# A two-lane recurrence in a transformer kernel: both lanes' levels in one go on TensorE, and a head's sum of squares beside the next head's output

## What is computed

```python
q = silu(q); f = lb + (1 - lb) * sigmoid(f_raw); k = 1 - f; v = i_in   # 8 heads of 128
S_t = diag(f_t) S_{t-1} + k_t v_t^T;   o_t = S_t^T q_t                 # all 272 tokens
o = o * rsqrt(mean(o * o) + 1e-6) * w_norm                             # per head
y_a = o * silu(g_out);  y_b = b_gate * dwconv(c_gate * x_conv)
h = h + (sigmoid(gate_a) * y_a + sigmoid(gate_b) * y_b) @ w_out
```

## Time and profile before

| | |
|---|---|
| median of 3 runs | 1136.73 us (1136.13 to 1136.94) |
| the profiled execution | 1137.76 us, its span 1136.5 us |
| TensorE | busy 1120.5 us (99%), 10518 matmuls |
| VectorE | busy 836.0 us (74%) |
| ScalarE | busy 633.2 us (56%) |
| granted TensorE clock | full in every slice after the first |
| stretch 743 to 760 us | TensorE busy 14.77 of 17, VectorE 12.95 |
| stretch 760 to 790 us | TensorE 30.00 of 30, VectorE 25.01, ScalarE 14.57 |
| stretch 790 to 812 us | TensorE 22.00 of 22, VectorE 16.54, ScalarE 13.23 |

### The profile page before, as it was taken

One profiled execution on the slowest core, in us unless ns is written; L12 is line 12 of the kernel. 1 busy time (PEld: TensorE's weight loads), 2 busy tenths in 40 slices (PEclk: granted clock), 3 DMA queues, 4 the chain that ended last, 5 costly groups with the idle time before them and its releaser, 6 DMA issues.

```text
span 1136.5 us, 24962 instructions
## 1 busy us (share of the span) xinstructions
PE 1120.5 (99%) x10518; PEld 1074.4 (95%) x10518; DVE 836.0 (74%) x1431; ACT 633.2 (56%) x1085; POOL 71.4 (6%) x96
## 2 busy tenths in 40 slices
PE   8999999999999999999999999999999999999998
PEld 5998899999998999999999999989999999999987
DVE  5688689988886888898575589577565777666643
ACT  3587556544444777666445456735645566555532
POOL 0200013000012000111000104100000000000000
PEclk9999999999999999999999999999999999999999
DMA  9977845899997634368755634733345463664540
GB/s 340 360 238 261 297 149 186 296 319 320 313 310 259 224 116 131 120 193 261 257 178 175 205 112 149 258 115 113 112 149 186 149 223 119 197 214 161 200 167 37
DMA packets 194671, 232.09 MB, mean 204 GB/s; under 512 B 4099, under 2 KB 169571, under 8 KB 194560
## 3 DMA queue, kind: packets, MB, share of 16 engines
q1 hardware_dynamic: 193712, 230.19, 60.9%
q0 software_dynamic: 576, 0.18, 0.1%
q10 hardware_dynamic: 272, 0.14, 0.0%
HBM read 229.43 MB, written 1.05 MB: 203 GB/s over the span
## 4 chain that ended last, share of the span: by engine, by line
PE 96%; DVE 3%; issue 1%; DMA 0%; ACT 0%; DVEq 0%; POOLq 0%
PE ps L154 94%; PE ps L157 2%; DVE hL L196 1%; DMA PI<-in_positions_dram 0%; DVE LT L187 0%; DVE T L196 0%; DVE wlo L187 0%; DVE T L187 0%; DVE ANG L196 0%; ACT hH L166 0%; DVE LT L193 0%; ACT LT L166 0%; DVE LT L196 0%; DVE hL L187 0%; DVE XA L192 0%
## 5 line engine op out<-in xcount | busy, mean ns | idle before, releaser
L187 DVE TENSOR_TENSOR wlo<-raw,whi 128x1024 fp32r<-128x1024 f32 (+1 forms) x346 | 408.6, 1204 | 154.0 <-ACT whi L166 152.7
L154 PE MATMUL ps<-hH,whi 128*128 128x256 f32 (+3 forms) x1792 | 516.2, 288 | 3.8 <-DVE hL L196 1.9
L154 PE MATMUL ps<-hL,whi 128*128 128x256 f32 (+3 forms) x1792 | 504.0, 281 | 0.0
L154 PE MATMUL ps<-hH,wlo 128*128 128x256 f32 (+3 forms) x1792 | 503.6, 281 | 0.4 <-DVE wlo L187 0.3
L166 ACT ACTIVATE whi<-raw 128x1024 fp32r<-128x1024 f32 (+1 forms) x346 | 348.8, 1033 | 185.8 <-PE ps L154 134.5
L154 PEld LDWEIGHTS ps<-hH,whi 128*128 128x128 f32 x1792 | 336.9, 188 | 10.8 <-issue 5.3
L154 PEld LDWEIGHTS ps<-hH,wlo 128*128 128x128 f32 x1792 | 337.1, 188 | 0.8 <-DVE wlo L187 0.8
L154 PEld LDWEIGHTS ps<-hL,whi 128*128 128x128 f32 x1792 | 337.4, 188 | 0.4
L154 PE MATMUL ps<-uL,whi 128*128 128x256 f32 x352 | 99.2, 282 | 0.0
L154 PE MATMUL ps<-uH,whi 128*128 128x256 f32 x352 | 99.0, 281 | 0.0
L154 PE MATMUL ps<-uH,wlo 128*128 128x256 f32 x352 | 98.4, 279 | 0.0
(11 more groups left out here) (321 smaller groups left out, 1600.3 us busy)
## 6 DMA issues: line engine op xcount, KB each, us to landing
MW<-in_w_mod_dram SPq DMA_DIRECT2D x47, 1024.0 KB, 6.6
raw<-in_w_up_dram SPq DMA_DIRECT2D x44, 1024.0 KB, 5.5
raw<-in_w_in_dram SPq DMA_DIRECT2D x36, 1024.0 KB, 5.0
raw<-in_w_down_dram SPq DMA_DIRECT2D x27, 1024.0 KB, 5.4
raw<-in_w_gate_dram SPq DMA_DIRECT2D x22, 1024.0 KB, 7.6
raw<-in_w_in_odd_dram SPq DMA_DIRECT2D x12, 1024.0 KB, 6.3
raw<-in_w_in_even_dram SPq DMA_DIRECT2D x8, 1024.0 KB, 6.2
raw<-in_w_down_dram SPq DMA_DIRECT2D x8, 768.0 KB, 6.8
```

Of the source, the lines that this page charges most:

```text
L154: return self.queued(self.e.matmul(out, lhsT, rhs, start=start, stop=stop, skip_group_check=True, **kw), length if pos is None else max(le ...
L187: return self.queued(self.e.tensor_tensor(out, a, b, op), 0.07 + cols(out) / self.RATE)
```

## The change

Level `lv` of lane 0 is queued only when lane 1 has also reached level `lv`, and lane 1's block follows it with no wide matmul between. `k.level` and its distance of 2.4 are gone. In the heads, `attended(h + 1)`, the output of the next head, is queued directly behind the sum of squares of head `h`; all four values `k.v` of the lane are awaited ahead of the first.

```diff
--- before.py
+++ after.py
@@ -2037,7 +2037,7 @@
         project(P.value[s], 0, value, s, s == 0)
     for s in range(4):
         project(P.query[s], 14, query, s)
-    k.level = 0.0
+    k.grown, k.begun_level = {}, set()
     lanes = [start(k, recur(k, i, VC)) for i in range(2)]
 
 
@@ -2182,9 +2182,16 @@
         wide = L2 if lv < 4 else 256
         b = banks[1 - lv % 2]
         ps = m.ps[b]
-        yield max(due(grown), read_out(k, b), k.level)
-        while pe.clock < k.level:
-            yield k.level
+        k.grown[lane, lv] = max(due(grown), read_out(k, b))
+        if lane == 0:
+            while (1, lv) not in k.grown:
+                yield None
+            yield max(k.grown[0, lv], k.grown[1, lv])
+        else:
+            while lv not in k.begun_level:
+                yield None
+            yield k.grown[1, lv]
+        k.begun_level.add(lv)
         fill(k, b)
         pe.wait_ge(*grown)
 
@@ -2204,7 +2211,6 @@
             for h in range(4):
                 pe.mm(ps[0:M0, 128 + h * 8:128 + h * 8 + 8], K[:, h, 256:272], later(Q[:, h, 256:272]), False, True)
         weights = pe.inc()
-        k.level = pe.clock + 2.4
         yield due(weights)
         yield from spare(k)
 
@@ -2269,18 +2275,23 @@
     weights = act.inc(k.bank[b1])
     yield due(weights)
     pe.wait_ge(*weights)
-    for h in range(4):
+    o = p0[:, 0:258]
+
+    def attended(h):
         j = 4 * lane + h
         V = m.VAB[:, :, j * 128:j * 128 + 128]
-        while k.v[j] is None:
-            yield None
-        o = p0[:, 0:258]
-        yield read_out(k, b0)
         fill(k, b0)
         pe.wait_ge(*k.v[j])
         pe.mm(o, V[:, 0, :], W[:, h, 14:272], True, False)
         pe.mm(o[:, 114:258], V[:, 1, :], W[:, h, 272:416], False, False)
-        out = pe.mm(o[:, 242:258], VC[:, j * 128:j * 128 + 128], CC[:, h, :], False, True).inc()
+        return pe.mm(o[:, 242:258], VC[:, j * 128:j * 128 + 128], CC[:, h, :], False, True).inc()
+
+    while None in k.v[hs]:
+        yield None
+    yield max(read_out(k, b0), due(*k.v[hs]))
+    out = attended(0)
+    for h in range(4):
+        j = 4 * lane + h
         yield due(out)
         OT, sq = m.T[:, j, 14:], SQ[h % 2]
         act.wait_ge(*out)
@@ -2288,9 +2299,11 @@
             act.wait_ge(*k.o[j - 2])
         square = act.act(sq, o, ACT.Square).inc()
         copied = act.act(OT, o, ACT.Copy).inc(k.bank[b0])
-        yield max(due(square), read_out(k, b1))
+        yield max(due(square, copied), read_out(k, b1))
         fill(k, b1)
         mean = pe.wait_ge(*square).mm(p1[:, 0:258], m.ones[:, 2, :], sq, True, True).inc()
+        if h < 3:
+            out = attended(h + 1)
         yield due(mean)
         act.wait_ge(*mean).act(sq, p1[:, 0:258], ACT.Ln, bias=m.eps[:, 1:2]).inc(k.bank[b1])
         rstd = act.settle().act(sq, sq, ACT.Exp, scale=-0.5).inc()
```

## The result

| | before | after |
|---|---|---|
| median, us | 1136.43 (4 runs, 1136.02 to 1136.94) | 1145.53 (4 runs, 1145.17 to 1148.93) |
| ratio, 95% interval | | 1.0079 (1.0066 to 1.0092) |
| profiled execution, us | 1137.76 (span 1136.5) | 1148.93 (span 1147.7) |
| mean granted clock of TensorE, share of full | 1.000 | 0.990 |

The change makes the kernel slower by 9.1 us in the medians and by 11.2 in the two spans. The forecast was 1137.4 us, with a range up to 1140.9. So the result lies outside, on the slower side.

What follows compares the result with a forecast made beforehand. TensorE, busy 1120.5 of 1136.5 us, was taken to bound the kernel. The terms 0 - 1.2 + 2.1 + 0.5 - 0.7 = +0.7 us, added to the median 1136.73, gave 1137.4 us, range 1133.6 to 1140.9.

Steps and rivals of the forecast that it cites:

- What bounds the kernel now: Whole kernel: TensorE bounds it, 96% of the chain; its two recurrence holes, 2.2 us, are it running out of instructions.
- The first instruction hole: Start of the recurrence: hole one and the first merge are gained, then given back waiting until 754.29; taken as 0.
- Merges: Level pairs: each saves a 0.20 us change into small fp32 matmuls and back; seven 1.4 us, the remaining six -1.2.
- VectorE: Level pairs: TensorE waits for both lanes' totals, 0.24, 0.96 and 0.94 us ahead of pairs 3, 4 and 5; +2.1 together.
- The walk: Pair-by-pair reckoning, from the profile's rows, of when VectorE's totals and TensorE reach each pair; it gave +2.1 us.
- the signs named: If right: one hole of 2 to 3 us, waits near 1 us at levels 4 and 5, VectorE's waits at 1-4 gone.
- Later holes: Recurrence past 754 us: a late fetch makes a hole near pair 3 or 4, mostly under VectorE's waits; +0.5, between 0 and 3.
- instruction starvation: Rival, chance 0.20: pairs outrun instruction fetch; two holes beyond the counted waits give +4 to +5, 1141 us.
- Heads: Heads: six sums of squares with an fp32 output behind them save 0.12 us each; -0.7, ends 0 and -1.2.
- Sum: All terms together: 0 - 1.2 + 2.1 + 0.5 - 0.7 = +0.7 us, added to the median, 1137.4 us.

Runs made afterwards that it cites:

- Spaced_only: The kernel before with the levels' distance of 2.4 modelled us also around each lane's own block, heads as before: 1135.18 us, 0.9985.
- heads_only: The kernel before with only the heads' change, a sum of squares together with the next head's output, levels as before: 1137.03 us, 1.0002.
- hole_wide: The kernel before with TensorE waiting once for nine GpSimd memsets amid wide matmuls near 850 us: 1140.5 us, 1.003.
- levels_only: The kernel before with only the change's level pairs, the heads as before: 1143.84 us, 1.0057.
- Load_late: The changed kernel with the weight load of 748 to 752 us held back until the pair of level 0 is done: 1140.56 us, 1.0036.
- pairs_kind: The changed kernel, pairs adjacent, with the weight load held back and 12 wide matmuls ahead of ab, ac and every head's step: 1139.25 us, 1.0022.
- spread: The changed kernel with 12 wide matmuls between lane 0's and lane 1's level blocks: 1142.76 us, 1.0044.
- tail_apart: As spread, with 12 wide matmuls also ahead of ab, ac and each head's output and sum: 1138.36 us, 1.0011.
- hole_small: The kernel before with TensorE waiting once for nine GpSimd memsets directly behind lane 0's block of level 3, near 766 us: 1139.75 us, 1.0029.
- hole_short: The kernel before with TensorE waiting once for four GpSimd memsets amid wide matmuls: 1138.02 us, 1.0009.

## Why the prediction was wrong, by its own steps

**What bounds the kernel now**: right as far as it went. TensorE's row sets the time, and the holes are missing instructions. Spaced_only shows the latter by what it does: with more wide matmuls between the small ones both holes go. The view I never put to use is the clock's. The table ahead has it at full, and I treated it as a constant of the kernel, though it depends on the order of the work, which was exactly what the change touched. Neither the sum nor any rival has a term for it. **This is the step that failed**: I took the wide matmuls to start 0.12 us apart throughout, and for 19.3 us they started 0.217 apart. That is 8.7 of 10.4 us in the profile, and by estimate 6 of 9.1 in the median.

**The first instruction hole** (taken as 0): right in time and length, in the profile. I had TensorE stop at 751.5 and resume at 754.29 after 2.8 us. It stopped at 752.28 and resumed at 754.88, 2.60 us, and these are 751.5 and 754.1 without the 0.76 that after starts late. The DMA queues show the weight load in front (packets, MB, share of 16 engines; window 750 to 751, then 752 to 752.6):

```profile
q1 hardware_dynamic: 372, 0.38, 108.0%
...
q1 hardware_dynamic: 161, 0.15, 77.6%
q8 instruction: 1, 0.02, 11.4%
```
The weights' queue holds over 100% of the engines' time from 750 on. The instructions' piece moves as its last packets do, and TensorE goes on some 2.3 us later, as in the earlier trace rows. But a hole of 2.6 us isn't worth the same as two holes of 1.28 and 0.95. The half clock begins inside it at 753.8 and lasts until 760.6. Behind the hole 5.7 us of it are left, and 5.7 x 0.45 = 2.6 us follow that before's two holes did not bring. The 0 was also reckoned against the holes of before's profile and then added to a median. Against an execution of before with one hole of 0.7 us, as in heads_only and hole_wide, the same step would cost some 1.5.

**Merges** (-1.4 for seven): right in size, rather low. A pair of 144 small matmuls takes 751.30 - 749.77 = 1.53 us from start to next start, where two blocks took 0.81 each and a change of 0.20 between. That saves 0.29 instead of 0.20. If every pair did so, the seven would be -2.0 and the clock's part of the 10.4 us would be 9.3.

**VectorE** (+2.1): the mechanism right, the size off, 0.8 measured. The walk made TensorE wait ahead of a *pair* for both lanes' totals. In fact lane 0's block starts with its own, and only lane 1's waits. In level 3 lane 0's block starts at 768.92 without waiting, and lane 1's at 770.20 after 0.41. The block in front takes 0.8 us of every wait I had walked. By that alone level 3's 0.24 would be nothing and level 4's 0.96 would be 0.2 or so. They are 0.41 and 0.37, because VectorE was also slower than in the walk. Its rows in after, its start on pair 2 (TensorE started that at 764.65) and lane 1's totals:

```profile
766.52 0.73 DVE L187 TENSOR_TENSOR Qg<-Qg,Fg 128x544 f32<-128x544 f32 x1
...
769.76 0.29 DVE L187 TENSOR_TENSOR LB<-Fg 128x136 f32<-128x136 f32 x1
```
It began 1.87 us behind the pair's start where I had 1.22, and the totals came after 5.40 where I had 4.58. Level 5's wait of 0.94 is absent, and TensorE had spent a hole of 1.22 us and 3.4 us at half clock on the way there. In levels_only, at full clock there, it is 0.39. Of the signs named, the waits stood at levels 3 and 4 with 0.4 us each, not at 4 and 5 with 1. VectorE's own waits vanished ahead of levels 2 to 4 but not ahead of level 1, where it stood 4.80 us, the first hole and the half clock behind it on the way.

**Later holes** (+0.5): mis-sized, 0.70 + 1.22 us measured. I had laid them under VectorE's waits, and they lie beside them. The rival of *instruction starvation*, with two holes beyond the counted waits, had the places right but priced a hole at its own length, 1141 us in all. Load_late shows what that rival is worth at the full clock: 4.6 us of holes, a span of 1137.4.

The Trainium skill (Runtime: NRT & Kernel Launch, Instruction fetch mechanics) calls crossing into the next block of instructions mostly hidden. By that rule all three holes of after, and both of before, would be nought. The runs show 2.2 us in before, 4.5 in after and none in spaced_only, so for blocks of small matmuls this close it doesn't hold.

**Heads** (-0.7): mis-sized, hardly anything measured (1.0002 with an interval of 0.001 either way; 1135.04 against 1135.18 us; 0.15 us between the heads of heads_only and before, matmul against matmul). And a cost that no step named: outputs and sums in one piece make the tail denser. Levels_only's profile has the full clock there, after's doesn't.

**Sum.** Of its terms 0 - 1.2 + 2.1 + 0.5 - 0.7 = +0.7, the profiles give about 0 - 1.2 + 0.8 + 1.9 - 0.2 = +1.3, and pairs_kind's recurrence +0.9. VectorE's term was 1.3 too high and that of the later holes 1.4 too low, and it is luck that they nearly cancel. Against the medians the sum was low even without the clock: pairs_kind is +1.9 at equal clock. So of the miss of 8.1 us (1145.5 against 1137.4) the missing term, the clock, is some 6. Another 1.2 is what pairs_kind shows beyond my sum. The last 1 us or so is open, and after's longest hole and its waits, of which pairs_kind has less, may be in it.

## What to carry to other kernels

Where TensorE sets the time and is near full use, an edit that moves small matmuls together is to be priced twice: by the holes it makes, and by the granted clock behind them, which is read from the clock column in windows and from the distance of two equal matmuls. The mean clock of each execution (here one thousandth was 1 us) tells it without a trace, and executions of two kernels are best compared at equal clock. One profile shows one execution: the holes of the same order were 2.2 us in one and 0.7 in another. In these runs small matmuls did best dealt out between wide ones; if a stretch must be dense, try it with 12 wide ones between steps before giving it up.

## What the runs showed of the hardware

- The granted clock falls to half without any idle time of TensorE: 10.2 us at 0.50 in spread, behind 44.4 us of unbroken work, where small fp32 steps stand three wide matmuls apart. With 12 ahead of each step (tail_apart's profile) it stays at 1.00. Three of spread's twelve executions kept 1.000 with the same tail. The Trainium skill (TensorE: Matmul & The Clock Gate, Why this matters for your kernels) warns of idle gaps between bursts of matmuls. By that alone this stretch would have kept its clock; here the measurement decides.
- Holes of 2.60 us (after), 2.40 (spread), 2.35 (levels_only) and 2.18 (hole_wide) had a stretch at half clock in or behind them, of 3.4 to 6.8 us. Holes of 2.18 (hole_small) and 2.02 (tail_apart) had none. One of 1.88 us in the same work had it in one of thirteen profiles. In before, hole_short and load_late, holes of up to 1.3 us had the full clock behind them; in after one of 1.22, close behind a wait of 0.37, had not.
- The change from one fp32 step of 128x258 to another costs the 0.2 us that I had ascribed to going from the wide fp32r matmuls to fp32 and back.
- For the same work a piece of instructions moved at 748.3 and 747.8 us, as a weight load began (heads_only, hole_wide), or at 751.9 behind that load (before), and only in the last TensorE then stood 0.95 us.
- A block of 144 small matmul records with their weight loads, 288 instructions, goes by in 1.53 us. That is more than the 256 of a piece, and load_late shows that a piece can come about 1 us too late behind it even with no weight load in its way.
